# Both prompt attentions ahead of both cached decodes in a hybrid decoder step on one core

## What is computed

```python
# sb, rows t over keys s < t
z = einsum('bthd,bshd->bhts', qb, k) * scale
ln1m = where(mask, log_sigmoid(-z), 0)
rc = cumsum(ln1m, axis=3, reverse=True)           # excl: rc moved by one key
a = where(mask, exp(log_sigmoid(z) + excl), 0);  out = einsum('bhts,bshd->bthd', a, v)
# fox, keys s <= t, C the cumulative log-forget
s = einsum('bthd,bshd->bhts', qb, k) * scale + C_q - C_k
out = einsum('bhts,bshd->bthd', softmax(where(mask, s, -inf)), v)
# after the mixers
o = concatenate([o_r * silu(g_r), o_s * silu(g_s), o_f * silu(g_f)]);  x = x + o @ w_out
x = x + (p @ w_pe) * sigmoid(rms_norm(x, g_pe) @ w_pg)
```

## Time and profile before

| | us |
|---|---|
| median of 3 runs | 3457.65 (3455.92 to 3467.43) |
| the profiled execution | 3443.23 |
| its span, first to last instruction | 3441.7 |
| TensorE busy | 3075.7 (89%) |
| VectorE, ScalarE, GpSimd busy | 1346.6, 942.9, 684.3 |
| DMA | 439.84 MB, mean 128 GB/s |
| mean granted TensorE clock | 0.937 of 2.4 GHz |

### The profile page before, as it was taken

The page is one execution under the profiler, slowest core; times in us unless marked ns, Lnnn a source line. Parts: engine busy times, 40 slices in busy tenths (PEclk is TensorE's granted clock), DMA queues, the critical chain, the costliest instruction groups (busy, mean ns, idle before and its releaser), DMA issues. The chain is left out here.

```text
span 3441.7 us, 67607 instructions
## 1 busy us (share of the span) xinstructions
PE 3075.7 (89%) x25160; PEld 1932.3 (56%) x25160; DVE 1346.6 (39%) x2894; ACT 942.9 (27%) x1740; POOL 684.3 (20%) x1234
## 2 busy tenths in 40 slices
PE   6999989788898889899989999897888997898997
PEld 4556656555575556544455566565556664665443
DVE  3225246454433455311242251555554245552211
ACT  2011234333224334211020122334432143441100
POOL 0000033245211036200000000332441110561000
PEclk9999999899899799999989999998989998999999
DMA  5111100688512279610130111007883123994111
GB/s 170 37 35 37 36 29 1 217 290 305 183 44 90 92 286 382 221 57 11 49 102 19 37 37 41 23 1 261 305 303 132 57 71 115 347 385 142 54 37 70
DMA packets 164260, 439.84 MB, mean 128 GB/s; under 512 B 48865, under 2 KB 77186, under 8 KB 163938
## 3 DMA queue, kind: packets, MB, share of 16 engines
q1 hardware_dynamic: 107554, 245.34, 20.6%
q0 software_dynamic: 54976, 186.63, 15.2%
q10 hardware_dynamic: 1536, 5.24, 0.4%
HBM read 410.41 MB, written 26.65 MB: 127 GB/s over the span
## 5 line engine op out<-in xcount | busy, mean ns | idle before, releaser
L930 PE MATMUL ps<-W,xT 128*128 128x320 f32 (+7 forms) x5120 | 1487.9, 465 | 12.2 <-DVEq L507 11.5
L930 PEld LDWEIGHTS ps<-W,xT 128*128 128x128 f32 (+1 forms) x5120 | 855.5, 184 | 579.3 <-issue 289.3
L785 POOL DMA_DIRECT2D branch<-in_cache_sb_v_dram x464 | 244.5, 527 | 339.1 <-issue 297.6
L1071 PE MATMUL ps<-branch 64*128 64x512 f32 (+7 forms) x480 | 209.4, 564 | 42.0 <-POOLq L507 19.5
L1196 PE MATMUL ps<-C,W 128*128 128x128 f32 x960 | 165.0, 324 | 72.1 <-DMA W<-in_cache_sb_k_dram 32.3
L1196 PEld LDWEIGHTS ps<-C,W 128*128 128x128 f32 x960 | 125.5, 164 | 133.5 <-issue 67.3
L1196 PE MATMUL ps<-C,branch 128*128 128x128 f32 x960 | 141.3, 288 | 47.3 <-DVE branch L2181 26.2
L785 POOL DMA_DIRECT2D branch<-in_cache_fox_v_dram x240 | 123.2, 514 | 282.6 <-issue 258.4
L1196 PEld LDWEIGHTS ps<-C,branch 128*128 128x128 f32 x960 | 107.1, 145 | 110.3 <-issue 56.0
L741 POOL DMA_DIRECT2D out_dram<-work x32 | 17.6, 550 | 744.6 <-ACT work L1465 550.5
L1648 ACT ACTIVATE W<-ps 128x512 f32<-128x512 f32 x224 | 131.1, 596 | 114.2 <-PE ps L1196 113.8
(11 more groups left out here) (260 smaller groups left out, 3831.5 us busy)
## 6 DMA issues: line engine op xcount, KB each, us to landing
branch<-in_cache_sb_v_dram POOLq DMA_DIRECT2D x464, 160.0 KB
xT<-in_cache_fox_k_dram SPq DMA_DIRECT2D x256, 160.0 KB
W<-in_cache_sb_k_dram SPq DMA_DIRECT2D x248, 160.0 KB
branch<-in_cache_sb_k_dram SPq DMA_DIRECT2D x240, 160.0 KB
branch<-in_cache_fox_v_dram POOLq DMA_DIRECT2D x240, 160.0 KB
W<-in_cache_fox_k_dram SPq DMA_DIRECT2D x128, 160.0 KB, 4.3
xT<-in_cache_fox_v_dram POOLq DMA_DIRECT2D x128, 160.0 KB
branch<-in_cache_fox_k_dram SPq DMA_DIRECT2D x120, 160.0 KB, 5.2
```

The costliest lines, as they stand in the source:

```text
L785: pool.dma_start(page_place(ring[n], p), page_of(CACHE[kind][1], L, pg))\
L930: ins = pe.matmul(out, src[:, k, t * P:t * P + R], W[W_OF[seg]][:, k, a:z], start=(k == 0), stop=(k == kc - 1), **place)
L1071: ins = pe.matmul(ps[:, 2 * (u % 2) + c // 512, 0:w], qT[q, a, t * P:(t + 1) * P], kT[q, a, c:c + w], start=True, stop=True)
```

## The change

Each layer's phases come in another order: ..., PROJ_S, ATT_S, PROJ_F, ATT_F, DEC_F, DEC_S, and then the output projection. Both decodes now use the same four key buffers and four value buffers, and the same twelve places for transposed blocks.

- fq, fk and fv are loaded in the common row of weight loads.
- The sb queries are stored to a DRAM scratch by GpSimd in PROJ_S, and brought back by SP in DEC_F, with the sb key rows; the sb value rows come back after DEC_F. TensorE waits for them (`rows_back`) at DEC_S's start and at its first last group.
- DEC_S's key groups 0 and 1 are issued by SP in fox's last sequence, ahead of fox's own last values; 2 and 3 when fox's last groups are weighed. Its value groups 2, 3, 0 and 1 are issued by GpSimd before it meets the others at DEC_F's end. ScalarE issues no keys for DEC_S.
- GpSimd does not wait for the stores of keys (`k_saved`) ahead of ATT_S, nor for any store ahead of ATT_F. ScalarE waits for them inside the attentions.
- The decoded rows of both kinds are loaded and multiplied in the output projection.

```diff
-LAST_VALUES = {"sb": {(SEQS - 2, 3): (0, 0), (SEQS - 1, 0): (1, 0), (SEQS - 1, 3): (0, 1)},
-               "fox": {(SEQS - 1, 3): (0, 0), (SEQS - 1, 2): (1, 0)}}
+LAST_VALUES = {"fox": {(SEQS - 1, 2): 2, (SEQS - 1, 3): 3}, "sb": {(SEQS - 1, 3): 0, (SEQS - 1, 2): 1}}
+def value_loads(kind, g):
+    return SEQS - ((SEQS - 1, g) in LAST_VALUES[kind])
...
-        ringK = {"sb": [spare[:, 0:PG8 * DA], in_branch[0]],
-                 "fox": [spare[:, 0:PG8 * DA], in_xT[0], in_xT[1], in_branch[0]]}
-        ringV = {"sb": in_branch[1:], "fox": [in_xT[2], in_branch[1], in_W0, in_branch[2]]}
-        kT_eight = [branch[:, PG8 * DA + n * 512:PG8 * DA + (n + 1) * 512] for n in range(5)] + \
-            [spare[:, PG8 * DA + n * 512:PG8 * DA + (n + 1) * 512] for n in range(SLOTS - 5)]
-        kT_d = {"sb": kT_eight + [W[0][:, g, :] for g in range(GROUPS)],
-                "fox": kT_eight + xT_rest + [W[0][:, g, :] for g in range(2)]}
+        key_buf = [spare[:, 0:PG8 * DA], in_xT[0], in_xT[1], in_branch[0]]
+        value_buf = [in_xT[2], in_branch[1], in_W0, in_branch[2]]
...
-        decoded = cut(work, 2880, SEQS, 2, HD)
+        decoded_of = {"fox": cut(work, 2880, SEQS, 2, HD), "sb": cut(work, 3904, SEQS, 2, HD)}
...
-        PROJ_R, RET, PROJ_S, ATT_S, DEC_S, PROJ_F, ATT_F, DEC_F = range(8)
+        PROJ_R, RET, PROJ_S, ATT_S, PROJ_F, ATT_F, DEC_F, DEC_S = range(8)
...
             def load_k(L, kind, b, g, pages_of_group=PG8):
-                cache = CACHE[kind][0]
                 s = dec[kind]
-                ring = ringK[kind]
-                n = g % len(ring)
-                if kind == "sb" and not (is_first(b) and g < 2):
-                    sp.wait_ge(s["kt_ready"], b * BLOCKS + 5 * (g - 1))
-                if kind == "fox" and not is_first(b):
+                if not is_first(b):
                     sp.wait_ge(s["kt_ready"], b * BLOCKS + 5 * (g + 1) - BLOCKS)
...
+            def decode_loads(L):
+                fox, stick = dec["fox"], dec["sb"]
+                sp.wait_ge(proj_ready, TILES * 12)
+                for g in EARLY_KEYS:
+                    load_k(L, "fox", 0, g)
+                sp.wait_ge(phase_sem, 4 * (ATT_F + 1))
+                load_k(L, "fox", 0, GROUPS - 1, PG8 - BY_ACT)
+                sp.wait_ge(fox["new_turned"], 1)
+                sp.dma_start(q_new[:], queries_dram).then_inc(rows_back, 16)
+                sp.dma_start(k_new[:], sbk_sample[L].rearrange("b s h d -> (b s) (h d)")).then_inc(rows_back, 16)
                 with sp.Fori(1, SEQS) as b:
                     for g in range(GROUPS):
-                        load_k(L, kind, b, g)
-                for b, g in LAST_VALUES[kind]:
-                    place, use = LAST_VALUES[kind][b, g]
-                    if use == 0:
-                        turned_blocks = 15 + 5 * place if kind == "sb" else 5 * (place + 1)
-                        sp.wait_ge(s["kt_ready"], (SEQS - 1) * BLOCKS + turned_blocks)
-                    else:
-                        sp.wait_ge(s["v_used"], 2 + (SEQS - 1) * GROUPS)
-                    for p, pg in enumerate(page_numbers(mybir.EngineType.SP, b * PAGES + g * PG8, PG8)):
-                        sp.dma_start(page_place(ringK[kind][place], p), page_of(CACHE[kind][1], L, pg))\
-                            .then_inc(s[f"k{place}"], 16)
-                sp.wait_ge(s["scores_done"], SEQS * SCORES)
-                if kind == "fox":
-                    sp.wait_ge(s["v_used"], (SEQS - 2) * GROUPS + 3)
-                load_weights(L, "fq" if kind == "sb" else "out0")
+                        load_k(L, "fox", b, g)
+                for g in range(2):
+                    sp.wait_ge(fox["kt_ready"], (SEQS - 1) * BLOCKS + 5 * (g + 1))
+                    load_k(L, "sb", 0, g)
+                load_last_values(L, "fox")
+                for g in range(2, GROUPS):
+                    sp.wait_ge(fox["v_used"], (SEQS - 1) * GROUPS + g + 1)
+                    load_k(L, "sb", 0, g)
+                sp.wait_ge(phase_sem, 4 * (DEC_F + 1))
+                sp.dma_start(v_new[:], sbv_sample[L].rearrange("b s h d -> (b s) (h d)")).then_inc(rows_back, 16)
+                with sp.Fori(1, SEQS) as b:
+                    for g in range(GROUPS):
+                        load_k(L, "sb", b, g)
+                load_last_values(L, "sb")
+                sp.wait_ge(stick["scores_done"], SEQS * SCORES)
+                sp.wait_ge(stick["v_used"], (SEQS - 2) * GROUPS + 3)
+                load_weights(L, "out0")
...
-                for seg in SEG_NAMES[2:9]:
+                for seg in SEG_NAMES[2:12]:
                     load_weights(L, seg)
-                decode_loads(L, "sb")
+                decode_loads(L)
                 sp.wait_ge(phase_sem, 4 * (DEC_S + 1))
-                load_weights(L, "fk")
-                load_decoded(L, "sb")
-                load_weights(L, "fv")
-                decode_loads(L, "fox")
-                sp.wait_ge(phase_sem, 4 * (DEC_F + 1))
...
+                pool.wait_ge(emptied_act, evac_count("sq", SAMPLE))
+                pool.dma_start(queries_dram, q_new[:]).then_inc(saved, 16)
+                stores += 1
                 for t in range(TILES):
                     src = k_new[:] if t == SAMPLE else nat[:, turn_index("sk", t) % 2, 0:DA]
                     store_kv("sk", t, src, sbk_prompt, sbk_sample, k_saved[t % 2],
                              emptied_act, evac_count("sk", t))
-                await_dma(k_saved[0], L * 160 + 16 * 5)
-                await_dma(k_saved[1], L * 128 + 16 * 4)
                 await_dma(saved, L * 16 * STORES + 16 * stores)
                 phase_over(pool, PROJ_S)
...
                 def load_values(kind):
+                    used = dec[kind]["v_used"]
+                    with pool.Fori(1, SEQS - 1) as b:
                         for g in range(GROUPS):
+                            await_dma(used, b * GROUPS + g + 1 - GROUPS)
+                            load_group(kind, b, g)
+                    for g in range(2):
+                        await_dma(used, (SEQS - 2) * GROUPS + g + 1)
+                        load_group(kind, SEQS - 1, g)
...
-                await_dma(k_saved[0], L * 160 + 16 * 10)
-                await_dma(k_saved[1], L * 128 + 16 * 8)
-                await_dma(saved, L * 16 * STORES + 16 * stores)
                 phase_over(pool, PROJ_F)
...
-                    issue_values("fox", 0, g)
+                    load_group("fox", 0, g)
                 phase_over(pool, ATT_F)
+                for g in (1, 3):
+                    load_group("fox", 0, g)
                 load_values("fox")
+                for g in (2, 3, 0, 1):
+                    await_dma(dec["fox"]["v_used"], (SEQS - 2 if g >= 2 else SEQS - 1) * GROUPS + g + 1)
+                    load_group("sb", 0, g)
                 phase_over(pool, DEC_F)
                 decoded_store("fox")
+                load_values("sb")
+                phase_over(pool, DEC_S)
+                decoded_store("sb")
...
             if kind == "sb":
-                    pe.sem_inc(s["v_used"], 2)
+                    pe.wait_ge(rows_back, 32)
...
+                if kind == "fox":
+                    act.wait_ge(k_saved[0], L * 160 + 16 * 10)
+                    act.wait_ge(k_saved[1], L * 128 + 16 * 8)
...
+                    if u == 0 and kind == "sb":
+                        act.wait_ge(k_saved[0], L * 160 + 16 * 5)
+                        act.wait_ge(k_saved[1], L * 128 + 16 * 4)
+                    elif u == 0:
+                        act.wait_ge(saved, (L + 1) * 16 * STORES)
...
-                bring_keys(1 if kind == "sb" else 3)
+                if kind == "fox":
+                    bring_keys(GROUPS - 1)
...
+                                link(gate_decoded("sb"))
...
-                dve.wait_ge(dec[kind]["loaded"], 16)
+                dve.wait_ge(loaded, 32)
...
                 attention(ATT_S, L)
-                decode(DEC_S, L)
                 project(PROJ_SEGS[PROJ_F])
-                link(gate_decoded("sb"))
                 phase_over(dve, PROJ_F)
                 attention(ATT_F, L)
                 decode(DEC_F, L)
+                decode(DEC_S, L)
```

131 lines of the change are left out of this document (49 added, 82 removed).

## The result

Before: 3456.78 us, median of 4 runs (3450.31 to 3467.43). After: **3366.55 us**, median of 4 runs (3361.45 to 3367.14). The ratio is 0.9733, with a 95% interval of 0.9706 to 0.9759: 90 us less. The profiled execution of after took 3361.45 us with a span of 3359.6.

A forecast was written before the change was run, and what follows sets the result against it. TensorE was taken to wait for key and value loads in DEC_S. The terms summed to -24.3 us per layer, -48.7 for both: 3394.5 us profiled, 3409 us as median with the 14.4 us difference, range 3388 to 3437.

The forecast's parts named there:

- the steady part: DEC_S, seven sequences from first to last fifths' scores: more buffers gain 32.5 us, 32.8 in the second layer.
- the 1.9 us for the fold: DEC_S: extra time per sequence over DEC_F for its longer fold, 1.9 us, 13.3 for seven.
- The prediction's own check: One DEC_S sequence: 35.4 us less load waits and slow transposes gives 29.3, against 27.4 + 1.9 = 29.3.
- DEC_F costed at nothing: Forgetting decode: the change was taken to leave its work and time as they are, 0 us.
- The first part of DEC_S: DEC_S's first sequence: key groups issued already in DEC_F, none by ScalarE, gain 6.5 us per layer.
- The new meeting: DEC_F to DEC_S: all wait for GpSimd's drain behind four more value groups, cost 13.0 us per layer.
- Rival 1: DEC_F to DEC_S: GpSimd's drain does not stretch, cost about 5 instead of 13.0 us, total 3393 us; chance 0.17.
- fq's wait: ATT_S to PROJ_F: TensorE waits for fq's weights, loaded only after fg's last matmuls, cost 3.4 us.
- The meetings before the attentions: Ahead of ATT_S and ATT_F: without GpSimd's store waits each comes 0.8 us sooner, gain 1.6 us per layer.
- Rival 4: Ahead of ATT_S and ATT_F, GpSimd's drain waits for stores anyway: 1.6 us lost per layer, 3412 us; 0.62 with the forecast.
- Rivals 2 and 3: In DEC_S: 2, collisions leave half the steady gain, 3442 us, 0.12; 3, the softening chain limits, 3474 us, 0.04.
- From span to median: Whole kernel: the median was 14.4 us above the profiled execution, and the same difference was assumed after the change.

## Why the forecast was too small, point by point

- **What bounds the kernel, and the steady part: right in kind.** The lead of the loads is the cause; taking it away brings the old time back. A steady sequence took 29.07 us (1271.44 to 1300.51), forecast 29.3. Of the terms, the 1.9 us for the fold was 1.7.
- **The step that failed is that DEC_F's time was taken for pure work: as the base of the subtraction, and as a stage that the change leaves at 0.** "With four and four buffers and the same loop as DEC_F, DEC_S should come to DEC_F's time" was worked out from the whole 196.6 us of the earlier trace rows. These contain DEC_F's stop, 5.0 us in layer 1 and 3.4 in layer 2, that has no copy in DEC_S. Five of the seven intervals of before are 27.4 us, and the 54.8 us for two stood in the earlier trace rows; seven times 27.38 is 191.7, and with 13.3 on top DEC_S would have come to 205.0, where 204.3 and 205.2 were measured. That alone is 9 us for both layers. The prediction's own check had it: 27.4 + 1.9 = 29.3 us a sequence is 205.1 for seven, a gain of 37.3 and not 32.5, and the two were not compared.
- **DEC_F costed at nothing: wrong, by 13 us.** 5.2 and 3.5 us of it are the interval with the stop, 3.0 and 0.6 the part behind the last fifths' scores (25.1 to 22.1 us in layer 1, at a clock of 0.92 instead of 0.83), the rest small differences. This could not be had from the diff; but one interval of 32.4 us among five of 27.4 was in the trace to ask about. That the stop is gone is shown; why the change takes it away is open.
- **The first part of DEC_S: right in kind, undersized.** 6.5 forecast, 9.6 and 6.7 measured. The early keys bring 5.8 and 5.3 of that. The 2.3 us put down to ScalarE's issues was a guess that no run here takes apart.
- **The new meeting: right, with errors that cancel by luck.** The forecast was an end 10.5 us behind the last issue; it was 7.0 (1127.13 to 1134.12). The traffic that the forecast reasoned with is not the difference: the last packet of q0 ended 4.5 us behind the last issue, 5.1 before. The remainder with nothing of GpSimd's moving was 2.5 us instead of 5.4, which stays open. But the issue itself ended later, since GpSimd stood 3.35 us for the place of sequence 6's group 3 (`v_used`), which my row of issues without a pause left out, and TensorE was done earlier, with a shorter last part. 13.0 became 14.8 and 14.3 (gaps of 15.6 and 15.1 instead of 0.8). Rival 1, a short drain and a term of about 5, is refuted. By the Trainium skill ("DMA: Bandwidth & Descriptors", "Anatomy of one DMA") the last transfer alone would take 2.4 us, an estimate, from which the prediction had a term of 4.9 us; the last packet ended 4.5 us behind the last issue here, and the drain 7.0, and of all drains behind value loads in these traces the shortest took 3.9 us.
- **fq's wait: right** (3.4; 3.4 and 3.7), and removable.
- **The meetings before the attentions:** 1.6 forecast, 2.7 measured, of which 1.8 are the waits. Rival 4, that the drain waits for the stores as well, is half true: without the explicit waits it lasts 2.27 us and not 0.78, but it costs less than wait and drain in a row. ScalarE's waits cost nothing: ATT_S took 153.5 us after and 153.7 before.
- **Rivals 2 and 3: refuted.** TensorE waits for no load in DEC_S, and the softening chain doesn't hold it up before its last sequence.
- **From span to median:** the forecast took off the 14.4 us by which before's profiled execution was under its median. After's is 5.1 under its own. These 9 us lie in the spread of before, and like the 9 us in stages that the change leaves alone they are chance and no merit or fault of the reasoning. The other differences of the account come to 25 us, and 3409 less 25 is 3384 us, still just under the range.
